# Turning the shifted chunks of a dilated pair's v on VectorE, so that near chunks load in one transfer a quadrant

## The reference, cut to what matters

```
offsets = [d * arange(-((w//2)//d), (w//2)//d + 1) for (w, d) in ((128,1), (512,4), (2048,16))]
s   = q_blk @ k_sel * scale            # per pattern, invalid keys masked
p   = softmax(s)
out = p @ v_sel                        # combined over patterns by their denominators
```

## Time and profile before

| | |
|---|---|
| Time before, median of 3 runs | 541.35 us (537.8 to 543.76) |
| The profiled execution's own time | 539.04 us |
| Its span, from first to last instruction | 537.3 us |
| Mean granted clock of TensorE | 0.981 |
| TensorE busy | 508.9 us, 95% |
| VectorE busy | 366.4 us, 68% |
| ScalarE busy | 244.6 us, 46% |
| GpSimd busy | 163.7 us, 30% |
| DMA moved | 99.75 MB, mean 186 GB/s |

### The profile page before, as it was taken

How to read it: one execution, slowest core, us unless ns; L and a number is a source line. 1 busy time by engine, 2 the same in 40 slices (tenths; PEclk the granted TensorE clock), 3 DMA queues, 4 the chain that set the end, 5 groups by cost and what they waited for, 6 DMA issues and landing times.

```text
span 537.3 us, 10125 instructions
## 1 busy us (share of the span) xinstructions
PE 508.9 (95%) x3902; PEld 410.3 (76%) x3902; DVE 366.4 (68%) x733; ACT 244.6 (46%) x483; POOL 163.7 (30%) x224
## 2 busy tenths in 40 slices
PE   8999999699799999999999999987989999999995
PEld 7888877587587777778888888766868777787884
DVE  6879787589786486621558968974998667653325
ACT  6712365246355565522543114642654655653224
POOL 0104232112023556533521223222212425664201
PEclk9999999799899999999999999997999999999998
DMA  8725789848879698999613367985698879999973
GB/s 293 279 78 135 153 214 225 172 94 178 200 178 212 139 252 202 222 236 292 147 41 98 99 137 177 225 172 115 151 227 177 206 174 274 232 209 248 227 181 156
DMA packets 61263, 99.75 MB, mean 186 GB/s; under 512 B 24480, under 2 KB 38304, under 8 KB 61216
## 3 DMA queue, kind: packets, MB, share of 16 engines
q0 software_dynamic: 19648, 62.93, 52.8%
q1 hardware_dynamic: 41280, 36.00, 23.0%
q10 hardware_dynamic: 288, 0.19, 0.1%
HBM read 84.92 MB, written 4.72 MB: 167 GB/s over the span
## 4 chain that ended last, share of the span: by engine, by line
PE 77%; DMA 7%; DVE 6%; issue 5%; POOL 2%; SPq 1%; ACT 1%; POOLq 0%; DVEq 0%; ACTq 0%
PE acc L625 17%; PE acc L626 16%; PE acc L627 16%; DMA sq<-sq 4%; PE sc L734 4%; PE tp L767 3%; PE misc L798 3%; DMA w_hi<-w_in 2%; PE misc L793 1%; PE sc L687 1%; DMA w_lo<-w_out 1%; PE sc L688 1%; PE sc L689 1%; SPq L505 1%; PE sc L625 1%
## 5 line engine op out<-in xcount | busy, mean ns | idle before, releaser
L625 PE MATMUL acc<-act_hi,w_hi 128*128 128x512 f32 x480 | 194.5, 405 | 0.0
L626 PE MATMUL acc<-act_hi,w_lo 128*128 128x512 f32 x480 | 187.6, 391 | 0.0
L627 PE MATMUL acc<-act_lo,w_hi 128*128 128x512 f32 x480 | 187.2, 390 | 0.0
L625 PEld LDWEIGHTS acc<-act_hi,w_hi 128*128 128x128 f32 x480 | 90.2, 188 | 21.9 <-issue 3.9
L627 PEld LDWEIGHTS acc<-act_lo,w_hi 128*128 128x128 f32 x480 | 90.2, 188 | 19.9
L626 PEld LDWEIGHTS acc<-act_hi,w_lo 128*128 128x128 f32 x480 | 90.3, 188 | 17.0 <-issue 0.5
L893 ACT ACTIVATE w_lo<-w_hi 128x1024 fp32r<-128x1024 f32 (+1 forms) x62 | 62.0, 1000 | 66.1 <-DMA w_hi<-w_out 39.1
L1318 DVE SCALAR_TENSOR_TENSOR y<-ub,par,y 128x512 f32<-128x512 f32 x90 | 68.5, 761 | 0.0
L1096 POOL DMA_DIRECT2D w_lo<-w_in x40 | 36.1, 901 | 100.2 <-ACT w_lo L893 99.6
L955 ACT ACTIVATE prob<-prob,nmx 128x384 f32<-128x384 f32 (+1 forms) x80 | 45.2, 565 | 45.4 <-DVE nmx L1340 45.4
L1318 DVE SCALAR_TENSOR_TENSOR ub<-ub,par 128x512 f32<-128x512 f32 x84 | 62.6, 745 | 0.0
(11 more groups left out here) (147 smaller groups left out, 720.7 us busy)
## 6 DMA issues: line engine op xcount, KB each, us to landing
w_hi<-w_in POOLq DMA_DIRECT2D x40, 512.0 KB, 5.9
w_lo<-w_in POOLq DMA_DIRECT2D x40, 512.0 KB, 6.1
w_hi<-w_out POOLq DMA_DIRECT2D x16, 512.0 KB, 6.2
w_lo<-w_out POOLq DMA_DIRECT2D x16, 512.0 KB, 6.6
pT<-w_in SPq DMA_DIRECT2D x15, 512.0 KB, 3.6
sq<-sq SPq DMA_DIRECT2D x48, 64.0 KB, 4.0
gf<-nabias SPq DMA_DIRECT2D x20, 128.0 KB, 5.6
v_way<-vs SPq DMA_DIRECT2D x32, 64.0 KB, 4.1
```

Source lines behind the costliest of these rows:

```text
L625: nc.tensor.matmul(to[:, :], w_hi[:, slot, k, :], a_hi[:, k, :], start=i == 0, stop=False)
L626: nc.tensor.matmul(to[:, :], w_lo[:, slot, k, :], a_hi[:, k, :], start=False, stop=False)
L627: last = nc.tensor.matmul(to[:, :], w_hi[:, slot, k, :], a_lo[:, k, :], start=False, stop=i == K - 1)
```

## The change: a second turn, and one near load for each quadrant

VectorE turns a dilated pair's v twice: the 4 even chunks of each class (128x512) and the 3 shifted ones (128x384), which it reads 16 tokens further on. Both go to vB, which grows from 512 to 896 columns, 7 chunks for each class in turn. `store_v` writes 896 columns for each partition to v_way (112 KB in each of four stores, 64 KB before). `load_v` then takes a quadrant's 7 near chunks in one load of 112 KB, and v_far in one as before: 8 loads a pair. Pair 1 no longer uses zs, so each turn waits for the store of the pair before it. Neighbourhood pairs move as before.

```
@@ -166,10 +166,10 @@
-        vs = sb("vs", [P, 2, SEQ])
-        vT, vB = vs[:, 0, :], vs[:, 1, :]
-
-        v_way = nc.dram_tensor("v_way", (DEPTH, PAIRS, BLK, P // BLK, SEQ), F32, kind="Internal").ap()
+        vs = sb("vs", [P, SEQ + CLASSES * NA_BLOCKS * BLK])
+        vT, vB = vs[:, 0:SEQ], vs[:, SEQ:]
+
+        v_way = nc.dram_tensor("v_way", (DEPTH, PAIRS, BLK, P // BLK, CLASSES * NA_BLOCKS * BLK), F32, kind="Internal").ap()
@@ -388,13 +388,12 @@
         def v_moves(g):
 
-            return 4 * QUADS if g < DPAIRS else QUADS
+            return 2 * QUADS if g < DPAIRS else QUADS
@@ -413,15 +412,13 @@
-        def v_buf(g):
-
-            return zs if g == 1 else vB
...
+        def by_chunk(t):
+
+            return t.rearrange("p (r m t) -> p r m t", r=CLASSES, t=BLK)
+
+        def v_columns(g):
+
+            return CLASSES * NA_BLOCKS * BLK if g < DPAIRS else SEQ
@@ -507,7 +504,8 @@
-                    sp.dma_start(v_way[l, g, :, i, :], v_buf(g)[BLK * i:BLK * (i + 1), :]).then_inc(v_stored, 16)
+                    n = v_columns(g)
+                    sp.dma_start(v_way[l, g, :, i, 0:n], vB[BLK * i:BLK * (i + 1), 0:n]).then_inc(v_stored, 16)
@@ -516,19 +514,14 @@
                     if g < DPAIRS:
-                        half = BLK // 2
-                        low = NEAR_ODD.stop - NEAR_ODD.start
-                        t = v_way[l, g].rearrange("p i (j c) -> j p i c", j=QUADS)
-                        sp.dma_start(to[:, :, NEAR_EVEN], t[j]).then_inc(v_moved[g % 2], 16)
-                        sp.dma_start(to[0:half, :, NEAR_ODD], t[j][half:BLK, :, 0:low]).then_inc(v_moved[g % 2], 16)
-                        sp.dma_start(to[half:BLK, :, NEAR_ODD], t[j][0:half, :, BLK:BLK + low])\
-                            .then_inc(v_moved[g % 2], 16)
-                        t = v_way[l, g].rearrange("p i (r j c) -> j p (i r) c", r=CLASSES, j=QUADS)[j]
+                        t = v_way[l, g].rearrange("p i (r c) -> r p i c", r=CLASSES)[j]
+                        sp.dma_start(to[:, :, :], t).then_inc(v_moved[g % 2], 16)
+                        t = v_way[l, g].rearrange("p i (r m c) -> m p (i r) c", r=CLASSES, c=BLK)[j]
                         sp.dma_start(v_far[BLK * j:BLK * (j + 1), g % 2].rearrange("p i (r c) -> p (i r) c", r=CLASSES), t)\
@@ -1255,11 +1248,17 @@
-                    before = {0: (l - 1, PAIRS - 1), 2: (l, 0), 3: (l, 2), 4: (l, 3)}.get(g)
-                    if before is not None and before[0] >= 0:
-                        dve.wait_ge(v_stored, V_STORED * (PAIRS * before[0] + before[1] + 1))
-                    nc.vector.transpose(v_blocked(g), vT.rearrange("p (m j t) -> p m j t", m=v_blocked(g).shape[1],
-                                                                         t=BLK)).then_inc(v_blocks, 1)
+                    before = PAIRS * l + g
+                    if before:
+                        dve.wait_ge(v_stored, V_STORED * before)
+                    if g < DPAIRS:
+                        nc.vector.transpose(by_chunk(vB)[:, :, 0:QT, :], vT.rearrange("p (r m t) -> p r m t", r=CLASSES, t=BLK))
+                        shifted = vT.rearrange("p (r a) -> p r a", r=CLASSES)[:, :, BLK // 2:P - BLK // 2]
+                        nc.vector.transpose(by_chunk(vB)[:, :, QT:NA_BLOCKS, :],
+                                            shifted.rearrange("p r (m t) -> p r m t", t=BLK)).then_inc(v_blocks, 1)
+                    else:
+                        nc.vector.transpose(vB[:, 0:SEQ].rearrange("p (z m t) -> p m z t", z=2, t=BLK),
+                                            vT.rearrange("p (m z t) -> p m z t", z=2, t=BLK)).then_inc(v_blocks, 1)
```

More of the change, by code:

```diff
@@ L390, in build @@
         QUADS = P // BLK
-        NEAR_EVEN, NEAR_ODD = slice(0, QT * BLK), slice(QT * BLK, NA_BLOCKS * BLK)
         V_STORED = 16 * QUADS
         def v_moves(g):
-            return 4 * QUADS if g < DPAIRS else QUADS
+            return 2 * QUADS if g < DPAIRS else QUADS
         def v_landed(l, g):
@@ L448, in p_turned @@
         def p_turned(q):
-            return (prob[:, 2:4, :], sq, vs, zc)[q][:, :, :].rearrange("p r t -> p (r t)")
+            return vs[:, 0:2 * SEQ] if q == 2 else (prob[:, 2:4, :], sq, None, zc)[q][:, :, :].rearrange("p r t -> p (r t)")
         def p_there(q):
@@ L530, in load_v @@
                         first = BLK * (j // 2)
-                        t = v_way[l, g].rearrange("p i (z c) -> z p i c", z=2)[j % 2]
+                        t = v_way[l, g, :, :, 0:SEQ].rearrange("p i (z c) -> z p i c", z=2)[j % 2]
                         t = t[:, :, first:first + BLK * NA_BLOCKS]
```

## The result

The changed kernel took 524.74 us (median of 4 runs, 521.53 to 526.17) against 540.85 us for the kernel before beside it (4 runs, 537.8 to 543.76): a ratio of 0.9694, 95% interval 0.9623 to 0.9766. By the ratio that is 16.5 us less, with 12.7 to 20.4 inside the interval; the medians differ by 16.1. The forecast was 521.3, a gain of 20.0, with a range of 516 to 531. The profiled execution took 526.17 us, span 524.4, at a mean granted clock of 0.998 (before: 537.3 and 0.981). It is the longest of the four.

The account below looks back on a forecast made before the run. TensorE was taken as the bound, its waits ahead of `values` set by SyncE's row of 16 load issues. 16.98 + 5.20 - 1.1 - 1.1 = 20.0 us off the median of 541.35 gave 521.3 us, range 516 to 531.

Parts of the forecast that it names:

- The bound and the term that matters: TensorE's waits ahead of `values` follow SyncE's 16 load issues a pair; eight fewer close them, 16.98 us.
- The clock: In the windows over `values` after the three long waits, the low clock goes: 5.20 us gained.
- The rule that speaks against it: The skill's statement that savings on the issuing side are usually small; by it the time stays at 541.
- The remainder of a wait: Ahead of `values`, three of four waits close narrowly; 1.1 us in all left for a remainder at one.
- rival A: Transfers, not issues, set the v loads' landing: 528 us, 531 with half the clock's share lost; chance 0.24.
- What is late next: VectorE trails by 1 to 3 us after pair 1; 2.3 us at the transposes and tap-free slots take it.
- rival B: VectorE becomes the bound, each of the four places costing 2 us of the gain: 529 us; chance 0.08.
- The second turn: VectorE's added turn takes 0.57 us; 1.1 us charged on pair 0's swap chain, hidden at pairs 1 and 2.
- The larger store: Stores of 112 KB a quadrant land 0 to 1.4 us later; 0.7 taken, counting at pair 1.
- The new waits of VectorE: VectorE's turn of a pair waits for the previous pair's store, already over by then: costed at nothing.
- C: No effect: v_moved doesn't end the waits, or the last landing follows the weight queue: 541 us; chance 0.05.
- D: Slower: denser loads hold the swap's landing ahead of TensorE's transposes, 12 us for each of two: 545 us; chance 0.03.

Follow-up runs that it names:

- Number 1: The changed kernel with each of its eight loads a pair cut in two, 16 issues again: 541.16 us, ratio 1.0026.
- Number 9: The kernel before without its two loads of shifted half chunks for each quadrant (8 loads a pair, one turn, 64 KB store): 519.57 us, ratio 0.9631.
- number 8: The changed kernel run once more with no edit: 522.85 us, ratio 0.9690 to the kernel before.
- number 2: The changed kernel without VectorE's second turn, the shifted chunks being zeros: 523.9 us, ratio 0.9681.
- Number 3: The changed kernel with only 2 of 8 slices of the weights of tiles 16 to 18 loaded: 517.51 us, ratio 0.9559.
- number 6: The changed kernel with one more VectorE turn of 128x512 for each dilated pair, into an unread buffer: 527.53 us, ratio 0.9763.
- number 5: The changed kernel with the store cut back to 512 columns (64 KB a quadrant), loads of the same count and bytes: 522.82 us, ratio 0.9688.
- number 4: The changed kernel with the near chunks of all four quadrants in one load, five loads a pair: 522.31 us, ratio 0.9650.
- number 7: The changed kernel with five loads a pair and convolution taps moved towards later slots: 522.74 us, ratio 0.9673.

## Why the prediction was right, and where it was off

**The bound and the term that matters: right.** Eight issues fewer end the wait ahead of `values`. Number 1 settles it: two turns, the large store, the same bytes and nearly the same packets, with 16 issues, have no gain at all (1.0026). New stretches of 4.2 to 6.2 us were expected, and 5.1 to 6.9 came. At layer 1's pair 0 one far load alone took 2.12 us to issue, so the upper bound was too low there. In layer 0 the last issue of pair 0 came 3.9 us earlier and not 5.9 (the 6.46 less the 0.57), since that profile's store of pair 0 started 1.97 us later than in the kernel before. Number 9, with one turn and the small store, has its first load there 2.7 us later as well (87.73), and number 8, with both, 1.3 us later (86.29), so the second turn isn't what shifts it.

**The clock: right for `values`, not for the rest.** The windows over `values` are at 1.00 and 2.8 us; the 5.20 us are all back. But the forecast counts no low clock behind other waits, and in number 8 there are 1.7 us of it behind the wait of 2.04 us at slot 9, of the length of the one that it counted as none.

**The rule that speaks against it: not refuted, but it doesn't cover this case.** The Trainium skill, "DMA: Bandwidth & Descriptors", section "Issuing engines are not separate DMA queues", says that the time a sequencer takes to initiate a DMA "is usually small relative to the DMA itself". For one DMA the trace agrees: in the changed kernel a far load takes 0.62 us to issue and 5.5 us to land, by the medians. The prediction made of it a rule for a row of 16 issues, and there it doesn't hold: the row took 10.6 to 13.2 us at the first two pairs, twice a landing, and taking half of it away was worth 16 us.

**The remainder of a wait, 1.1 us: mis-sized.** The step compared TensorE's arrival with a landing 5.4 to 6.9 us after the last issue, and took these three as the range. The landing can come up to 9.2 us after, and then 3.9 us remain (number 2: 3.5 us, at the other layer). In number 8 nothing remains, and that the 1.1 charged lies between the two is luck. The late landing is rival A's mechanism at one of four places in some executions. Number 3 has no late load and points to the weight traffic, but number 8 with full weights has none either, so single profiles don't prove it. (Rival A's own sum counts the 0.57 us of the turn twice at each pair 0, in the arrival and in the 1.1; without that it comes to 527 us and not 528.)

**What is late next: mis-sized, the step that failed most.** I charged 1.1 us for the swap's chain and let the trailing of VectorE be absorbed by the 2.3 us of slack at the transposes. The waits for pT grew from 2.3 to 6.4 and 6.2 us, 4.1 and 3.9 more, and the low clock behind one of them added 1.7 in number 8. By place, in the first profile and in number 8:

- Between the `values` of pairs 0 and 1, 2.6 and 1.9 us. TensorE now comes earlier, k waits for its swap, and VectorE, with no slack, passes that on in full (the table above). TensorE's early arrival alone does nothing: in number 3 it comes to pair 1 at 128.14, earlier still than the 133.92 of the changed kernel, k is in time, and there is no wait.
- At the transposes of slot 9, 0.1 and 1.5 us. The swap's chain was named rightly as having nothing to spare; in number 8 its landing took 6.85 us and not 5.55.
- Ahead of all of pair 0's loads, near 74 and 82 us, 1.5 and 0.5 us. Nothing there was moved by the loads: number 9 has a wait of 2.77 us at that place and number 6 one of 1.37, so executions differ there by as much, and no share of the change is shown.

Number 8 misses the forecast span, 537.3 - 20.0 = 517.3, by 2.9 us. Its terms give 3.4: 3.9 for pT less the 1.1 charged, and 1.7 of clock, less the 1.1 of the other remainder, which it doesn't have. So rival B was partly real, at 4 us and not at the 8 it was priced with, and its cause was the late k together with the full VectorE, more than the added turn.

**The second turn: its duration right, its price wrong.** 0.536 us measured, 0.57 estimated. The 1.1 us charged at pair 0 is not shown by any run. At pairs 1 and 2 it was held to be hidden, and by the table above it isn't where k is late: it adds 0.8 to 1.2 us a layer to the waits. The times don't decide it: number 2 is no faster than the changed kernel, number 9 is 3 us faster.

**The larger store, 0.7 us: right to be small, wrong in how.** The stretch from pair 1's store to its first load grew by 2.6 us in layer 0 (5.49 to 8.11) and 2.1 in layer 1 (5.41 to 7.47), beyond the bound of 1.4. Size alone isn't the cause: in layer 0 the small store of number 5 took 7.37 us and that of number 9 8.13, and under light weights the large one took 3.65. In layer 1 the small one took 5.53 in number 5 and 7.31 in number 9, so a part for the size isn't excluded. That TensorE's earlier pace puts the store beside other weight transfers would explain it and is not shown. The delay was hidden, as no profile of the kernels with eight loads has a wait for the loads at pair 1.

**The new waits of VectorE: right.** No turn of v waits for a store in the changed kernel. One wait for a store did appear, 0.9 us at L1351, where a turn of probabilities into `vs` waits for the layer's last pair. It isn't the change's own: number 9, with the buffers of before, has 0.5 us there. What brings it is not shown.

**The rivals C and D are out as forecasts of the time**: landings followed the issues, and pair 0's swaps landed in 6.06 and 5.54 us in the first profile, against 5.55 and 5.98 before. A late swap does occur (6.85 us in number 8, 8.10 in number 6), as D has it, but not at the 10 us and more that it needed, and that denser loads cause it is not shown.

**A better version.** Five loads (number 4) has the lowest ratio of those that compute everything, 0.9650, and no wait for the loads in its profile (number 7, with the same loads, has one of 0.6 us); but the changed kernel's own intervals, 0.9623 to 0.9766 and 0.9639 to 0.9742, hold it. It is not shown to be faster.

## What to carry to other kernels

When a wait follows the last of a row of small transfers, take first issue to last issue and compare it with one landing: if the row is longer, fewer and larger transfers are worth their full difference, and extra work to make them possible is cheap as long as its engine keeps slack. A wait that is closed takes away the time in which other engines had been catching up, so their slack must be read after the shift and not before: here VectorE then passed each late k on to TensorE, 2 to 3 of the 22 us. Three landings are no range: leave a margin at each place for a later one. And read the clock behind every wait of 2 us or more, not only at the place where it was low before.

## What was not expected of the hardware

The same kernel has the last load of a pair land in time in one execution and 9.2 us after its issue in another (TensorE resumes after 9.33), with weight transfers on GpSimd's queue started 0.8 us ahead and 1.8 us behind that issue. The Trainium skill, "DMA: Bandwidth & Descriptors", section "Queues, rings and completion order", has each DMA engine take turns between the queues with work, a packet at a time. No run here shows these turns. They don't by themselves bound a small load's landing: the far loads landed 3.5 to 9.2 us after their issue in the changed kernel (the tile v_far, last line of its view), and with the bytes of three weight tiles cut, in number 3, both remainders were absent.

```profile
DMA to landing us min/median/max: 3.5/5.5/9.2
```

The clock does not follow the length of the idle time alone: after 3.89 us of TensorE's idle time the granted clock stayed at 1.00 (changed kernel, 356.76), and after 3.50 us it fell to the 1.2 GHz level (number 2, windows):

```profile
97.37:100.86 3.49, 0.00 (x0) 0.03 (x1) 3.46 (x10) 2.16 (x4) 0.39 (x1) 1.00 0.78 220
100.86:103.70 2.84, 2.84 (x56) 2.84 (x60) 1.04 (x3) 0.00 (x0) 0.48 (x1) 0.50 0.70 131
```

That alone is 1.7 us. Shorter waits did it too: after 2.04 us in number 8, 2.30 in number 4 and 2.40 in number 5 the clock fell to the 1.2 GHz level and cost 1.7 us each time, while after 2.77 us in number 9, 2.48 in number 1 and 2.04 in the kernel before it stayed at 1.00. So a wait of 2 us and more may cost 1.7 us on top or not. Issues of one shape also differ: a load of 448 KB with all 128 partitions as its destination took 0.34 to 0.53 us to issue, one of 112 KB 0.54 to 1.35 us in the changed kernel.
